# Norm gains of keys, values, queries and gate multiplied into the weight split, one transposed x for four products

## Chip, core and metric

The kernel runs on one core of a Trainium2 chip. The metric is the device time of one execution in microseconds, taken as the median of several runs. Five engines work side by side, each through its own list of instructions in order: TensorE (PE in the profile, its weight loads PEld), VectorE (DVE), ScalarE (ACT), GpSimd (POOL) and SyncE (SP, which here only starts transfers). They wait for each other through semaphores.

## Reference

Two blocks of a decoder are computed one after the other, on 256 tokens of width 1024. The part that the change touches is the second layer of the first block: keys and values come from one normed x, queries and gate from another. Both norms divide the same x by the same root mean square, and differ only in the gain vector.

```python
def rms_norm(x, g):
    xf = x.astype(jnp.float32)
    y = xf * lax.rsqrt(jnp.mean(xf * xf, axis=-1, keepdims=True) + EPS)
    return (y * g.astype(jnp.float32)).astype(x.dtype)
...
            kv_in = rms_norm(x, kv_norm)
            k_all, v_all = jnp.split(kv_in @ w_kv, 2, axis=-1)
            k_sh = rms_norm(split_heads(k_all), k_norm)
            v_sh = split_heads(v_all)
            h = rms_norm(x, b_norm[j])
            q, z = jnp.split(h @ b_w_in[j], 2, axis=-1)
            q = rms_norm(split_heads(q), b_q_norm[j])
            o = stick_breaking_attention(q, k_sh, v_sh)
            x = x + (o * jax.nn.silu(z)) @ b_w_out[j]
        x = x + (p[i] @ ple_w[i]) * jax.nn.sigmoid(x @ ple_gate_w[i])
```

After it come the second block's two attentions (called moba and mla), an MLP, a state-space mixer and a second MLP.

## The kernel before

**Split products.** Each large product runs as three matmuls (lines 591, 592, 593): high part of the activations times high part of the weights, high times low, low times high. A weight block of 1024 x 512 arrives in the tile ring in two halves, of 128 x 2048 each (four slabs of 128 input rows by 512 columns). For each half ScalarE writes the high part (whi, line 1035), VectorE then subtracts it from the block and writes the low part (wlo, line 1356). Both have three buffers (PARTS), so half g can be made when TensorE is done with half g-3. A half is 24 matmuls. The helper refill(name, half) in the two engines' lists makes the half that lies three ahead of the one named; the refill stands in the list between other work, and its place there sets the order. The wait first_used says that TensorE is done with a block's first half, low_made that a half is ready for TensorE.

**Transposed activations.** turn() has TensorE transpose x, two chunks of 128 columns and both token tiles to a unit, four units to a tensor (line 584). ScalarE reads a unit's bank and writes hT_hi (line 1018 with a gain as its scale, line 1015 without), VectorE reads the same bank and writes hT_lo (line 1347). Four such tensors of units stand in the stage at hand: "kv" (x with kv_norm), "qz" (x again, with b_norm), then "k" and "q" (the normed keys and queries of the heads, copied out by both engines in turn, lines 1006 and 1336). The order on TensorE is: turn kv, products k and v, turn qz, turn k, product q, product zb (the gate), turn q, then stick-breaking attention. The reciprocal root mean square is applied to the products as they are copied out (line 993), so the transposed x holds the gain alone.

**Head norms.** For keys, and later for queries, VectorE squares (line 1575), sums (line 1580) and finishes the mean, GpSimd takes the power (rsh, line 1855), VectorE scales (line 1585) and signals heads_normed. The chain stands in VectorE's list behind the low part of the second half of block v1 (for keys) or zb1 (for queries), and ahead of the next two refills.

**Banks.** There are eight PSUM banks. The class Units writes the plan: each result unit takes the next bank in turn (or a fixed one where the attention loops name it), and records which unit held the bank before and which engine empties it. TensorE waits for that in begin(). A unit more or less in the plan therefore shifts the bank of every later unit that is numbered in turn, against those with a fixed bank. Fixed banks are used by the units of the three attention loops: stick-breaking (logits and loga in 0 to 5, stick_out in 6 and 7), moba and mla (scores in 0 to 3, probsT in 4 and 5, soft_out in 6 and 7). The MLP takes its f1 units from banks 4 to 7 in turn and its sums from 0 to 3.

## Time and profile before

| | |
|---|---|
| median of 3 runs | 1003.29 us (1002.31 to 1003.59) |
| the profiled execution | 1003.81 us |
| its span, first to last instruction | 1002.0 us |
| PE busy | 910.1 us, 91% |
| DVE busy | 577.8 us, 58% |
| ACT busy | 440.2 us, 44% |
| mean granted TensorE clock | 0.951 of 2.4 GHz |

The stage at hand runs from about 134 us (turn kv) to 238 us (first logits). Stick-breaking attention ends at 284 us, moba starts at 396 us, mla at 432 us, the first MLP at 476 us. A timeline row gives start, duration, engine, line, operation, output and inputs, count of merged instructions, and in brackets how long the engine had been idle before and who released it. Consecutive instructions overlap a little, so that of a merged row the duration divided by the count is the distance at which one follows the other.

### The profile page before, as it was taken

What the parts mean: (1) busy time and instruction counts of PE and PEld (TensorE: products, weight loads), DVE (VectorE), ACT (ScalarE), POOL (GpSimd) and SP (SyncE); (2) the same over time, 40 slices, a digit from 0 to 9 for tenths busy, and PEclk for the clock granted to TensorE, in tenths of its full rate; (3) what the DMA queues carried; (4) which work ended last, traced back from release to release, by engine and by line L of the source; (5) the groups of instructions that cost most, each with busy time, mean ns of one, the idle gap of its engine ahead of it and who ended that gap; (6) DMA issues with size and microseconds to landing.
All of it is one profiled execution on the core that took longest, in us unless ns stands there. A gap on an engine that the chain in (4) does not pass through costs nothing.

```text
span 1002.0 us, 11908 instructions
## 1 busy us (share of the span) xinstructions
PE 910.1 (91%) x4907; PEld 750.9 (75%) x4907; DVE 577.8 (58%) x754; ACT 440.2 (44%) x552; POOL 134.2 (13%) x72
## 2 busy tenths in 40 slices
PE   3999999898999999999999999996519989999998
PEld 3888778786887886787788888875517878888886
DVE  3585465654244675767677777762482464545553
ACT  4443564555743646254444444422305454444441
POOL 1000000101000011213044444440020000000000
PEclk9999999997999999599999999997857999999999
DMA  9526555451023643206355555479525655555531
GB/s 351 195 85 210 185 202 200 139 197 43 1 79 126 220 146 118 107 22 210 126 189 200 189 200 189 158 116 106 157 116 210 186 168 180 182 190 188 171 124 42
DMA packets 66783, 155.84 MB, mean 156 GB/s; under 512 B 2937, under 2 KB 6618, under 8 KB 66474
## 3 DMA queue, kind: packets, MB, share of 16 engines
q1 hardware_dynamic: 64000, 145.89, 45.4%
q0 software_dynamic: 2224, 7.67, 2.2%
q10 hardware_dynamic: 506, 1.52, 0.4%
q8 instruction: 39, 0.64, 0.3%
q14 instruction: 14, 0.11, 0.0%
HBM read 146.69 MB, written 7.34 MB: 154 GB/s over the span
## 4 chain that ended last, share of the span: by engine, by line
PE 81%; DVE 10%; ACT 3%; issue 2%; DMA 2%; POOL 2%; ACTq 0%; SPq 0%; POOLq 0%
PE bank L591 22%; PE bank L593 22%; PE bank L592 21%; POOL rsh L1855 2%; PE bank L584 2%; DVE wlo L1356 2%; PE bank L686 1%; PE bank L845 1%; PE bank L715 1%; DMA vrows<-in_vecs 1%; PE bank L930 1%; PE bank L960 1%; DVE aux L1810 1%; DVE aux L1812 1%; PE bank L727 1%
## 5 line engine op out<-in xcount | busy, mean ns | idle before, releaser
L1356 DVE TENSOR_TENSOR wlo<-ring,whi 128x2048 fp32r<-128x2048 f32 (+1 forms) x122 | 288.4, 2368 | 208.6 <-ACT whi L1035 208.6
L1035 ACT ACTIVATE whi<-ring 128x2048 fp32r<-128x2048 f32 (+1 forms) x124 | 236.8, 1911 | 274.0 <-PE bank L593 239.4
L591 PE MATMUL bank<-whi,hT_hi 128*128 128x512 f32 (+1 forms) x736 | 290.9, 395 | 9.3 <-DVE hT_lo L1347 7.3
L593 PE MATMUL bank<-whi,hT_lo 128*128 128x512 f32 (+1 forms) x736 | 288.1, 391 | 0.0
L592 PE MATMUL bank<-wlo,hT_hi 128*128 128x512 f32 (+1 forms) x736 | 288.0, 391 | 0.0
L591 PEld LDWEIGHTS bank<-whi,hT_hi 128*128 128x128 f32 x736 | 139.7, 190 | 38.6 <-DVE hT_lo L1347 5.8
L593 PEld LDWEIGHTS bank<-whi,hT_lo 128*128 128x128 f32 x736 | 139.5, 190 | 28.9
L592 PEld LDWEIGHTS bank<-wlo,hT_hi 128*128 128x128 f32 x736 | 139.8, 190 | 27.7
L591 PE MATMUL bank<-whi,hidT_hi 128*128 128x512 f32 x256 | 100.7, 393 | 1.1 <-DVE hidT_lo L1753 1.1
L593 PE MATMUL bank<-whi,hidT_lo 128*128 128x512 f32 x256 | 99.8, 390 | 0.0
L592 PE MATMUL bank<-wlo,hidT_hi 128*128 128x512 f32 x256 | 99.6, 389 | 0.0
L591 PEld LDWEIGHTS bank<-whi,hidT_hi 128*128 128x128 f32 x256 | 48.0, 188 | 12.5 <-issue 2.9
L593 PEld LDWEIGHTS bank<-whi,hidT_lo 128*128 128x128 f32 x256 | 48.0, 188 | 10.2
L592 PEld LDWEIGHTS bank<-wlo,hidT_hi 128*128 128x128 f32 x256 | 48.1, 188 | 9.8
L1244 ACT ACTIVATE aux<-bank 128x512 f32<-128x512 f32 x32 | 19.2, 599 | 45.9 <-PE bank L593 45.9
L1855 POOL TENSOR_TENSOR rsh<-msh,half_neg 128x16 f32<-128x16 f32 (+1 forms) x6 | 22.5, 3742 | 125.6 <-DVE msh L1581 125.6
L1851 POOL TENSOR_TENSOR rstd<-ms,half_neg 128x2 f32<-128x2 f32 x4 | 2.8, 707 | 267.9 <-DVE ms L1371 267.9
L993 ACT ACTIVATE work<-bank,rstd 128x512 f32<-128x512 f32 (+1 forms) x32 | 21.8, 686 | 34.2 <-PE bank L593 34.1
L960 PE MATMUL bank<-ring,aux 64*32 64x128 f32 x256 | 11.4, 415 | 27.9 <-DVE aux L1819 27.9
L1760 DVE TENSOR_TENSOR aux<-bank,aux 128x512 f32<-128x512 f32 x32 | 22.0, 688 | 18.8 <-ACT aux L1244 18.8
L960 PEld LDWEIGHTS bank<-ring,aux 64*32 64x32 f32 x256 | 10.0, 166 | 29.1 <-DVE aux L1819 28.1
L1483 DVE TENSOR_TENSOR aux<-pb,bb 128x512 f32<-128x512 f32 x16 | 27.6, 1762 | 0.0
(244 smaller groups left out, 1016.2 us busy)
## 6 DMA issues: line engine op xcount, KB each, us to landing
ring<-in_w_ff SPq DMA_DIRECT2D x64, 1024.0 KB, 5.3
ring<-in_a_w_in SPq DMA_DIRECT2D x8, 1024.0 KB, 8.3
ring<-in_ple_gate_w SPq DMA_DIRECT2D x8, 1024.0 KB, 5.0
ring<-in_w_kv SPq DMA_DIRECT2D x8, 1024.0 KB, 6.5
ring<-in_b_w_in SPq DMA_DIRECT2D x8, 1024.0 KB, 5.0
ring<-in_w_glu SPq DMA_DIRECT2D x8, 1024.0 KB, 6.0
ring<-in_w_in SPq DMA_DIRECT2D x6, 1024.0 KB, 5.8
ring<-in_a_w_out SPq DMA_DIRECT2D x4, 1024.0 KB, 5.1
```

Source lines behind the costliest of these rows:

```text
L584: last = pe.transpose(b[0:width, cc * S + t * P:cc * S + t * P + P], src[:, t, c * width:(c + 1) * width], ident)
L591: pe.matmul(bank_cols, high[:, at[0], at[1]], w_high, start=first, stop=False)
L592: pe.matmul(bank_cols, high[:, at[0], at[1]], w_low, start=False, stop=False)
L593: return pe.matmul(bank_cols, low[:, at[0], at[1]], w_high, start=False, stop=last)
L960: last = pe.matmul(b[32 * q:32 * q + 32, s * P:(s + 1) * P], states[rows, 0:NC, 8 * m + 4 * r + s], wr[rows, 8 * q + 4 * r + s, :], start= ...
L993: act.activation(dst, b[:, :] if src is None else src, func, scale=scale).then_inc(act_emptied, 1)
L1035: act.activation(whi[at], ring[:, slot[name], cols], ACT.Copy).then_inc(high_made, 1)
L1244: act.activation(hid[:, t, :], b[:, :], ACT.Relu).then_inc(relu_ready, 1)
L1356: dve.tensor_tensor(wlo[at], ring[:, slot[name], cols], whi[at], ALU.subtract).then_inc(low_made, 1)
L1483: dve.tensor_tensor(at[:, 4 * r:4 * r + 4], ai[:, 4 * r:4 * r + 4], other, ALU.mult)
L1760: dve.tensor_tensor(hid[:, t, :], b[:, :], hid[:, t, :], ALU.mult).then_inc(dve_emptied, 1)
L1855: pool.tensor_tensor(rsh[:, 0:n], msh[:, 0:n], half_neg[:, 0:n], ALU.pow).then_inc(headr_ready, 1)
```

## The change

The gains kv_norm and b_norm are no longer applied to the transposed x but to the weights as they are split: row r of a weight block is multiplied by entry r of the gain. In a half, each slab of 512 columns has a gain column of its own, so one instruction on 128 x 2048 becomes four on 128 x 512, on ScalarE (scale operand) and on VectorE (scalar_tensor_tensor: block times gain minus high part) alike. This is done for the 16 halves of k, v, q and zb. Since the transposed x then holds no gain, the units of "qz" go (16 transposes on TensorE, 8 activations, 8 VectorE instructions), and q and zb use the transposed "kv", which is copied without a gain.

```diff
@@ plan()
     gemm(u, "v", 2, "a")
-    turned_in_two(u, "qz")
     turned(u, "k")
@@ tensor engine
-            turn("qz", x)
             turn("k", k_tok, ready=lambda k: pe.wait_ge(heads_normed, 1))
             for nb in range(2):
-                product("q", nb, ("q", nb), turned_by="qz")
+                product("q", nb, ("q", nb), turned_by=None)
@@ shared
+        gained = {"k": "kv_norm", "v": "kv_norm", "q": "b_norm", "zb": "b_norm"}
@@ scalar engine, fill(g)
+                if name[0] in gained:
+                    for kk in range(4):
+                        n = slice(512 * kk, 512 * kk + 512)
+                        ins = act.activation(whi[at][:, n], ring[:, slot[name], cols][:, n], ACT.Copy,
+                                             scale=gain(gained[name[0]], 4 * (g % 2) + kk))
+                    ins.then_inc(high_made, 1)
+                    return
                 act.activation(whi[at], ring[:, slot[name], cols], ACT.Copy).then_inc(high_made, 1)
...
-            turned_high("kv", "kv_norm")
+            turned_high("kv", None)
...
-                if nb:
-                    turned_high("qz", "b_norm")
                 tokens_out("v", nb, v_tok, 1)
@@ vector engine, fill(g)
+                if name[0] in gained:
+                    for kk in range(4):
+                        n = slice(512 * kk, 512 * kk + 512)
+                        ins = dve.scalar_tensor_tensor(out=wlo[at][:, n], in0=ring[:, slot[name], cols][:, n],
+                                                       scalar=gain(gained[name[0]], 4 * (g % 2) + kk),
+                                                       in1=whi[at][:, n], op0=ALU.mult, op1=ALU.subtract)
+                    ins.then_inc(low_made, 1)
+                    return
...
-            turned_low("kv", "kv_norm")
+            turned_low("kv", None)
...
             refill(("v", 1), 0)
-            turned_low("qz", "b_norm")
             turned_out("k", [(kT, "k_norm", True)])
```

On TensorE, between the end of product v and the start of product q, there stood before (first the transposes of x, then those of the normed keys, then the first matmul of q; a bracket lists the semaphores waited for):

```order
L584 MATMUL bank<-cst,x 128x128 [waits act_emptied]
L584 MATMUL bank<-cst,x 128x128 x3
...
L584 MATMUL bank<-cst,work 128x128 [waits heads_normed,act_emptied]
L584 MATMUL bank<-cst,work 128x128 x3
...
L591 MATMUL bank<-whi,hT_hi 128x512 [waits low_made,dve_emptied]
```

and stands now (line 584 is 585 there, 591 to 593 are 592 to 594; the first row is the last matmul of v):

```order
L594 MATMUL bank<-whi,hT_lo 128x512
L585 MATMUL bank<-cst,work 128x128 [waits heads_normed,act_emptied]
L585 MATMUL bank<-cst,work 128x128 x3
...
L592 MATMUL bank<-whi,hT_hi 128x512 [waits low_made,act_emptied]
L593 MATMUL bank<-wlo,hT_hi 128x512
```

The transposes of x are gone, and product q no longer waits for VectorE's reading of them.

At the end of stick-breaking attention, where the output is transposed for b_out, TensorE's list read before (line 741 is the last matmul of stick_out 3):

```order
L741 MATMUL bank<-work,aux 128x64
L584 MATMUL bank<-cst,h 128x128 [waits dve_emptied,act_emptied]
L584 MATMUL bank<-cst,h 128x128 x3
...
L584 MATMUL bank<-cst,h 128x128 [waits dve_emptied]
L584 MATMUL bank<-cst,h 128x128 x3
L591 MATMUL bank<-whi,hT_hi 128x512 [waits low_made,dve_emptied,act_emptied]
```

and reads now:

```order
L741 MATMUL bank<-work,aux 128x64
L585 MATMUL bank<-cst,h 128x128 [waits dve_emptied]
L585 MATMUL bank<-cst,h 128x128 x3
L585 MATMUL bank<-cst,h 128x128 [waits dve_emptied,act_emptied]
L585 MATMUL bank<-cst,h 128x128 x3
...
L592 MATMUL bank<-whi,hT_hi 128x512 [waits low_made,dve_emptied,act_emptied]
```

The same four units are transposed; their banks, and with them the waits, are others. The four units fewer in the plan shift the banks by four at these places (bank: unit that held it before, and the engine that empties it):

| unit | before | now |
|---|---|---|
| T k 0 to 3 | 3 to 6: v (ACT) | 7, 0, 1, 2: k (ACT) |
| q 0,0 and 0,1 | 7, 0: T qz 0, 1 (DVE) | 3, 4: v 0 (ACT) |
| T o1 0 | 3: loga 15 (ACT) | 7: stick_out 3 (DVE) |
| T o1 1 to 3 | 4, 5, 6: loga 10, 11 (ACT), stick_out 2 (DVE) | 0, 1, 2: loga 12, 13, 14 (ACT) |
| moba scores 0 | 0: ukv 1,1 (ACT) | 0: uq 1,1 (ACT) |
| moba scores 1 to 3 | 1, 2, 3: uq (ACT) | 1, 2, 3: ukv 0,0 to 1,0 (ACT) |
| mla scores 0 | 0: T kmla 3 (ACT) | 0: T qmla 3 (ACT) |
| mla scores 1 to 3 | 1, 2, 3: T qmla 0, 1, 2 | 1, 2, 3: T kmla 0, 1, 2 |
| first f1, token tile 0 | 4: T ffn 3 (DVE) | 4: w_o 1,1 (DVE) |
| first f1, token tile 1 | 5: w_o 0,0 (DVE) | 5: T ffn 0 (DVE) |

T ffn 0 to 3 are the transposed x of the first MLP, f1 its first product; ukv and uq are the small products ahead of moba.

## Rows read from the trace of the kernel before

**Rows 1.** The page: busy time of the engines, share of the span, instructions.

```profile
PE 910.1 (91%) x4907; PEld 750.9 (75%) x4907; DVE 577.8 (58%) x754; ACT 440.2 (44%) x552; POOL 134.2 (13%) x72
```

**Rows 2.** Groups by form, ACT: form, count, busy us, mean ns, idle before.

```profile
L1035 ACT ACTIVATE whi<-ring 128x2048 fp32r<-128x2048 f32 x122 | 233.6, 1916 | 270.6 <-PE bank L593 236.0 <-DMA ring<-in_w_glu 9.0 <-DMA ring<-in_ple_gate_w 8.8
L993 ACT ACTIVATE work<-bank,rstd 128x512 f32<-128x512 f32 x30 | 20.6, 692 | 33.7 <-PE bank L593 33.6
...
L993 ACT ACTIVATE aux<-bank 128x512 f32<-128x512 f32 x12 | 7.2, 598 | 21.4 <-PE bank L930 15.9 <-PE bank L686 5.5
```

**Rows 3.** Groups by form, DVE, the same columns.

```profile
L1356 DVE TENSOR_TENSOR wlo<-ring,whi 128x2048 fp32r<-128x2048 f32 x120 | 284.7, 2376 | 206.2 <-ACT whi L1035 206.2
...
L1777 DVE SCALAR_TENSOR_TENSOR x<-bank,inv,x 128x512 f32<-128x512 f32 x8 | 6.0, 751 | 16.7 <-PE bank L593 16.7
...
L1396 DVE SCALAR_TENSOR_TENSOR aux<-aux 128x64 f32<-128x64 f32 x1 | 0.2, 225 | 0.0
L1439 DVE TENSOR_TENSOR aux<-aux 128x64 f32<-128x64 f32 x1 | 0.2, 225 | 0.0
```

**Rows 4.** Timeline of DVE ahead of product k.

```profile
130.92 2.29 DVE L1356 TENSOR_TENSOR wlo<-ring,whi 128x2048 fp32r<-128x2048 f32 x1 [2.12 <-ACT whi L1035]
133.13 0.68 DVE L1550 TENSOR_TENSOR sig<-sig,aux 128x512 f32<-128x512 f32 x1
...
134.99 0.69 DVE L1550 TENSOR_TENSOR sig<-sig,aux 128x512 f32<-128x512 f32 x1 [0.45 <-ACT sig L1108]
```

**Rows 5.** The chain that ended last, 135 to 240 us: start, duration, what.

```profile
135.71 0.70 DVE x L1557
...
164.94 1.93 ACT whi L1035
166.89 2.29 DVE wlo L1356
...
181.76 4.40 DVE wlo L1356 x2
186.16 1.58 DVE hT_lo L1347 x4
187.83 0.47 PE bank L591
...
215.40 1.93 ACT whi L1035
```

**Rows 6.** Timeline around the end of stick-breaking attention.

```profile
284.41 1.92 PE L584 MATMUL bank<-cst,h 128*128 128x128 f32 x16
284.61 0.69 DVE L1624 TENSOR_TENSOR h<-bank,work 128x512 f32<-128x512 f32 x1 [3.68 <-PE bank L741]
```

**Rows 7.** Timeline, start of moba, then of mla.

```profile
391.54 3.60 PE L786 MATMUL bank<-ring,aux 128*128 128x512 f32 x8
...
396.06 0.48 PE L801 MATMUL bank<-pT,sig 64*128 64x128 f32 x2 [0.93 <-ACT work L1206]
...
428.98 2.62 DVE L1336 TENSOR_SCALAR work<-bank,vcols 96x256 f32<-96x256 f32 x6 [0.51 <-PE bank L584]
432.04 0.49 PE L801 MATMUL bank<-work 96*128 96x128 f32 x2 [0.92 <-ACT work L1006]
```

**Rows 8.** Timeline, start of the first MLP: DVE, then PE.

```profile
473.02 3.23 DVE L1347 SCALAR_TENSOR_TENSOR hT_lo<-bank,vcols,hT_hi 128x256 fp32r<-128x256 f32 x8 [0.62 <-ACT hT_hi L1018]
...
476.30 0.80 PE L591 MATMUL bank<-whi,hT_hi 128*128 128x512 f32 x1 [2.69 <-DVE hT_lo L1347]
```

**Rows 9.** Stretches: us, then busy (count) of PE, PEld, DVE, ACT, POOL, PEclk, DMA share, GB/s.

```profile
181.00:188.00 7.00, 4.19 (x34) 3.57 (x33) 7.00 (x8) 6.36 (x13) 0.00 (x0) 1.00 0.39 128
...
237.40:247.60 10.20, 9.95 (x32) 7.48 (x33) 1.80 (x4) 5.33 (x11) 0.00 (x0) 0.50 0.31 104
...
472.90:476.30 3.40, 0.71 (x8) 0.47 (x6) 3.23 (x8) 3.40 (x8) 0.00 (x0) 0.99 0.59 241
476.30:479.70 3.40, 3.40 (x8) 2.72 (x9) 2.55 (x3) 2.85 (x5) 0.00 (x0) 0.51 0.00 0
```

## The prediction

> **What bounds the kernel.** I read the page first: TensorE is busy for 910.1 of 1002.0 us [rows 1], so a gain of 2 us has to come from time in which TensorE stands still or runs at its lower clock, or from instructions taken off it. The 16 transposes taken away are 1.75 us of it. Then the chain that ended last, for the stage that changes [rows 5]: it leaves TensorE three times. Ahead of k it runs through the last update of x (135.71 + 0.70). From 164.94 it runs through the high and low part of the second half of v1, the head norm of the keys, the low parts of q's two halves, and two units of hT_lo, to the first matmul of q at 187.83. From 215.40 it runs through the same for the queries, up to the logits. So in this stage VectorE and ScalarE set two of the three stretches, and work added to them is not hidden there. Elsewhere there are three buffers: a half takes TensorE 5.5 us (five of them from 187.83 to the release at 215.40 [rows 5]), so the next one in a buffer is due 11 us after its release, and is made in 1.93 + 2.29 us [rows 5]: there, added work is hidden up to some 6 us. Last I read what TensorE waits for where the banks shift: the ends and starts of the attention loops and the first MLP [rows 6 to 8].
>
> **The dearer split.** High part: one instruction of 1.92 us on 2048 columns becomes four on 512 with a gain as scale. The nearest row is the copy-out with a scale from a tile, 0.692 us on 512 [rows 2]; back to back it overlaps by about 0.09, so four take some 2.5 us: a = 0.6 us more. Bounded below by the 512 without a scale, 0.598, four in 2.07: 0.15 more; above by no overlap, 2.77: 0.85. Low part: four of the form "times a column, then with a tensor", 0.751 us on 512 [rows 3], overlap 0.08: 2.8 us against 2.29, d = 0.5 us more. Below: if the form cost no more than a plain 512 of 0.68 [rows 4], four in 2.5, 0.2 more; above without overlap, 3.0: 0.7.
>
> The row of 0.751 reads one operand from a bank, where the changed instruction reads both tensors from SBUF. The one pair of rows for that is small: on 64 columns, both from SBUF, this form took 225 ns, and the plain two-tensor form 225 ns too [rows 3], so at that size there is no sign of a lower rate. The Trainium skill, "Vector Engine (DVE) Microarchitecture Reference", section "Points that are easy to get wrong", speaks against this change: the form with two SBUF sources that are not bf16 runs at half the throughput. By that page each low part would take about twice as long; the trace does not agree at 64 columns, and shows no larger case. It is the second rival below.
>
> **The stage, step by step** (positive is later than before).
> 1. Before k: the low part of k0's second half, 130.92 to 133.21, stands ahead of the gate work [rows 4]. It starts a later and lasts d longer. Of that 0.54 was slack, since without the wait for ScalarE the instruction of 134.99 could have started at 134.45. So x is ready, and product k starts, at a + d - 0.54 = 0.56 later. The copies of "kv" without gains get cheaper, but nothing waits for them.
> 2. Products k and v run without a gap: each half is made in 5.3 instead of 4.2 us and due after 11. The second half of v1 is released 0.56 later and costs a + d = 1.1 more; the head norm behind it is as before. heads_normed comes 1.66 later, at 183.4.
> 3. TensorE ends v near 181.9 (the release at 164.94, three halves more, and 0.56) and stands until 183.4; it transposes k in 1.9 us, as 16 transposes took in [rows 6], to 185.4. q's first half is low at 181.76 + 1.66 + 2.8 = 186.1, and q starts at 186.3. Before, its low part was ready at 184.0 but q waited for the second unit of hT_lo until 187.83, its banks having been those of qz 0 and 1. So q starts 1.5 to 1.6 **earlier**: in symbols 2a + 3d - 4.28.
> 4. Products q and zb run through. The second half of zb1 starts 1.56 earlier, costs 1.1 more, and the norm of the queries behind it is as before: the logits start 3a + 4d - 4.28 = **0.5 earlier**. From the low bounds of a and d it is 3.0 earlier, from the high ones 1.1 later.
>
> So the folding itself is almost given back. TensorE's 1.75 us of transposes were done in time in which it would have waited.
>
> **The banks.** Four units fewer move all later ones.
> 5. End of stick-breaking: T o1 0 now takes the bank of stick_out 3. TensorE started it at 284.41, right behind its last matmul, while VectorE reads that bank from 284.61 to 285.30 [rows 6]. It now waits for 285.4: **1.0 later**; nothing behind it has slack, since T, ScalarE's high and VectorE's low part follow one another.
> 6. Start of moba: the first scores waited 0.93 for ScalarE to empty ukv 1,1, until 396.02, though the last ukv was done at 395.14 [rows 7]. They now need uq 1,1, whose matmuls lie ahead of the first ukv at 391.54. ScalarE's next work needs the first maximum, and VectorE's needs these scores, so the whole chain moves: **0.9 earlier**.
> 7. Start of mla: the first scores waited for ScalarE to empty T kmla 3, until 432.0, 0.92 after the transposes had ended. They now need T qmla 3, four units earlier in ScalarE's list, and T kmla 0, which VectorE ends with the fourth of its six instructions from 428.98, at 430.7 [rows 7], before the last transpose: **0.8 earlier**.
> 8. First MLP: f1 waited for the bank of T ffn 3, so for all 8 instructions of hT_lo, 473.02 to 476.25, and started at 476.30 after 2.69 idle [rows 8]. It now needs T ffn 0 alone, two of them, ready at 473.9; the next unit comes at 474.7 and is due at 475.3. Its weights are ready, their low parts standing ahead of the eight in VectorE's list. **2.3 earlier**. What ScalarE and VectorE do next for f1 is released by TensorE's own matmuls, so nothing takes this back.
> 9. The clock: at 473 to 476.3 TensorE was busy for 0.7 of 3.4 us, and in the next 3.4 us it was granted 0.51, the lower level of 1.2 GHz [rows 9]. Without the wait there is no such lull. At half speed for 3.4 us it lost **1.7**.
>
> Sum for the profiled execution: -0.5 + 1.0 - 0.9 - 0.8 - 2.3 - 1.7 = -5.2, 1003.8 - 5.2 = 998.6 us (its span is 1002.0, and 1.8 lie around it, unchanged). The median is 1003.3, 0.5 below the profiled execution; whether the lower clock fell at 476 in all runs is not known, so against the median I take it at two thirds: 1003.3 - 3.5 - 1.1 = 998.7. I predict **998.7 us**.
>
> **Rivals.**
> - *The bank gains do not arrive* (10%). Were something else due just behind at steps 6 to 8, only the folding and step 5 would be left: 1003.3 - 0.5 + 1.0 = 1003.8, and with one of the three 1000.4 to 1003. For it: moba and mla are chains over three engines with small waits everywhere. Against: the named releaser was the last to come in each, and idle time stood on all engines.
> - *The low part at half rate* (4%), the one that ends slower. Per column the plain low part takes 1.1 ns (2.29 us on 2048), so a piece would take 0.751 + 0.55 = 1.3 us, four 5.0, d = 2.7. Then step 4 gives 1.8 + 10.8 - 4.28 = 8.3 later instead of 0.5 earlier: 998.7 + 8.8 = 1007.5. It decides from d = 1.8 on, where the gain of the banks is used up. VectorE would be busy for 5.0 of each 5.5 us in k to zb.
> - *The clock falls at the keys' transposes* (5%). TensorE is busy for only 1.9 of the 4.4 us from 181.9 to 186.3. Before, it was busy for 4.19 of 7 us there and kept the full clock [rows 9]. A lower stretch lasted 3.4 or 10.2 us in this trace and would cost 1.7 to 5: 1000.4 to 1003.7.
> - *Cheap pieces* (8%): with the low bounds of a and d the folding brings 3.0 instead of 0.5: 996.2.
>
> **Numbers.** The forecast with its own spread (a and d between bounds, the clock at step 9 lost or not) holds 73% and spans 996.9 to 1000.6. The range of eight in ten reaches over the cheap pieces and a bank gain that is missing in part: 996.2 to 1001.2. A change under 0.2% (2 us) is about what a measurement of this kernel cannot tell from none. Below 1001.3 lie the forecast, the cheap pieces and part of the clock's and the banks' case: faster 0.85. Within 0.2% most of the rest of these: 0.11. Slower: 0.04.
>
> **What would show it.** High parts of k to zb in groups of four, about 2.5 us, low parts about 2.8; product q starting near 186.3, the logits 0.5 us earlier than before; the transposes of o1 with an idle time of 1.0 released by VectorE's h; no wait for ScalarE at the first scores of moba and mla; f1 starting 0.4 us after the transposes, with the full clock behind it. The forecast is wrong if the low part takes over 4 us, if TensorE's idle time at f1 stays at 2 us or more, or if the PEclk row falls between 182 and 190 us.

## The result and the profile after

| | before | after | predicted |
|---|---|---|---|
| median | 1002.92 us (1002.31 to 1003.59, 4 runs) | 995.71 us (995.03 to 996.31, 4 runs) | 998.7 (996.2 to 1001.2) |
| ratio | | 0.9929 [0.9902, 0.9956] | 0.9954 |
| profiled execution, its span | 1003.81, 1002.0 | 996.31, 994.5 | 998.6 for the profiled one |

The change is faster, as forecast, but by 7.2 us and not by 4.6, and so 0.5 us below the range. In words first: the steps at the stage itself and at the banks came out nearly as worked out, but for the clock. In the profiled pair a further 3.3 us were gained 450 us behind the change, in the state-space mixer, where the prediction had looked for nothing. Why TensorE lost time there before is shown below by experiment; how much of it the medians hold is not.

The page after (answers [rows 1]): TensorE has 16 instructions fewer and is busy 2.2 us less.

```profile
PE 907.9 (91%) x4891; PEld 749.5 (75%) x4891; DVE 581.2 (58%) x794; ACT 446.9 (45%) x588; POOL 134.3 (13%) x72
```

Groups by form after (answers [rows 2, 3]; form, count, busy us, mean ns of one, idle before it). The 16 halves are now 64 pieces on each engine. A piece of the low part, both tensors in SBUF, takes 747 ns, where the same form with one operand in a bank took 751.

```profile
L1369 DVE TENSOR_TENSOR wlo<-ring,whi 128x2048 fp32r<-128x2048 f32 x104 | 248.1, 2389 | 170.6 <-ACT whi L1042 170.6
L1042 ACT ACTIVATE whi<-ring 128x2048 fp32r<-128x2048 f32 x106 | 202.9, 1916 | 244.9 <-PE bank L594 207.0 <-DMA ring<-in_ple_gate_w 12.2 <-DMA ring<-in_w_glu 10.5
...
L1364 DVE SCALAR_TENSOR_TENSOR wlo<-ring,vcols,whi 128x512 fp32r<-128x512 f32 x64 | 43.7, 747 | 31.2 <-ACT whi L1038 31.1
L1038 ACT ACTIVATE whi<-ring,vcols 128x512 fp32r<-128x512 f32 x64 | 40.9, 712 | 22.0 <-PE bank L594 22.0
```

The timeline of VectorE ahead of product k (answers [rows 4]): the low part of k0's second half now takes 2.74 us instead of 2.29 and starts 0.40 later, and the gate work behind it no longer waits for ScalarE.

```profile
131.32 2.74 DVE L1364 SCALAR_TENSOR_TENSOR wlo<-ring,vcols,whi 128x512 fp32r<-128x512 f32 x4 [2.28 <-ACT whi L1038]
...
135.30 0.68 DVE L1563 TENSOR_TENSOR sig<-sig,aux 128x512 f32<-128x512 f32 x1
136.02 0.69 DVE L1570 TENSOR_TENSOR x<-x,sig 128x512 f32<-128x512 f32 x1
```

The chain that ended last (answers [rows 5]; start, duration, what). The same road as before: the split of the second half of v1, the head norm, one half of q low, then product q, at 187.55. The step through hT_lo is gone.

```profile
166.85 2.57 ACT whi L1038 x4
169.45 2.74 DVE wlo L1364 x4
172.19 2.21 DVE aux L1588
...
182.46 2.29 DVE work L1598
184.75 2.66 DVE wlo L1364 x4
187.41 0.14 issue
187.55 0.47 PE bank L592
...
215.38 2.57 ACT whi L1038 x4
```

The end of stick-breaking attention (answers [rows 6]), the starts of moba and mla ([rows 7]) and of the first MLP ([rows 8]), four pieces of timelines. T o1 now waits for VectorE's h, 0.79 of idle time. The first scores of moba and of mla and f1 start right behind the work in front of them.

```profile
284.27 0.69 DVE L1636 TENSOR_TENSOR h<-bank,work 128x512 f32<-128x512 f32 x1 [3.68 <-PE bank L741]
285.02 1.97 PE L585 MATMUL bank<-cst,h 128*128 128x128 f32 x16 [0.79 <-DVE h L1636]
```

```profile
392.21 3.60 PE L786 MATMUL bank<-ring,aux 128*128 128x512 f32 x8
395.74 0.49 PE L801 MATMUL bank<-pT,sig 64*128 64x128 f32 x2
```

```profile
428.82 1.91 PE L585 MATMUL bank<-cst,work 128*96 128x128 f32 x16
430.56 0.39 PE L801 MATMUL bank<-work 96*128 96x128 f32 x2
```

```profile
469.91 2.10 PE L585 MATMUL bank<-cst,x 128*128 128x128 f32 x16
472.44 0.47 PE L592 MATMUL bank<-whi,hT_hi 128*128 128x512 f32 x1 [0.43 <-DVE hT_lo L1352]
```

The stretches (answers [rows 9]; busy us and count of PE, PEld, DVE, ACT, POOL, then PEclk, DMA share, GB/s). Behind 473 the clock now stays full. Behind 138.0, at the start of product k, it is at 0.52, the lower level, which it was not before.

```profile
134.60:138.00 3.40, 1.48 (x13) 1.25 (x11) 3.33 (x8) 1.56 (x4) 0.00 (x0) 0.98 0.81 255
138.00:141.40 3.40, 3.40 (x9) 2.62 (x8) 1.78 (x6) 3.40 (x7) 0.00 (x0) 0.52 0.14 54
...
469.60:473.00 3.40, 2.97 (x22) 2.33 (x21) 2.27 (x6) 2.45 (x7) 0.00 (x0) 1.00 0.87 277
473.00:476.40 3.40, 3.40 (x16) 2.80 (x15) 2.63 (x6) 3.40 (x5) 0.00 (x0) 1.00 0.08 34
```

**Where the time went.** I took marks on TensorE at which both traces do the same thing, and subtracted the lengths between them (us, profiled executions):

| from, to | before | after | difference | forecast |
|---|---|---|---|---|
| start, second half of T kv | 136.55 | 136.86 | +0.31 | +0.56 |
| to the first matmul of q | 51.28 | 50.69 | -0.59 | -2.1 |
| to the first logits | 49.82 | 51.18 | +1.36 | +1.1 |
| to T o1, its wait included | 46.76 | 46.29 | -0.47 | +1.0 |
| to the first probsT of moba | 115.88 | 114.95 | -0.93 | -0.9 |
| to T o2, behind mla | 48.08 | 46.82 | -1.26 | -0.8 |
| to the middle of the first MLP | 42.18 | 38.32 | -3.86 | -4.0 |
| to the regrouping in the state-space mixer | 194.06 | 194.01 | -0.05 | 0 |
| to line 960, in the same mixer | 63.55 | 60.23 | **-3.32** | 0 |
| to TensorE's last wait, 15 us before the end | 238.82 | 240.12 | +1.30 | 0 |

In the row of T o1 the new wait is inside, but the low stretch at the start of attention was 10.2 us long before (237.4 to 247.6, [rows 9]) and 6.8 us after (240.3 to 247.1), which gives back about 1.6. After, 3.4 us more at the lower level stand ahead of this row, at 233.5 to 236.9, in the transposes of the queries. They cost nothing in the row of the first logits: from q to the logits it is 51.18 us in spare16, which has such a stretch, and 51.22 in all_three, which has none (both kernels stand below). The one large row that the forecast has at nothing is the state-space mixer.

**What is in that row.** TensorE's timeline at line 930, before:

```profile
701.50 0.66 PE L916 MATMUL bank<-cst,aux 128*128 128x128 f32 x4
702.09 0.95 PE L930 MATMUL bank<-work 128*32 128x128 f32 x7
707.15 3.64 PE L930 MATMUL bank<-work 128*32 128x128 f32 x25 [4.12 <-issue]
```

and after:

```profile
697.31 1.99 PE L930 MATMUL bank<-work 128*32 128x128 f32 x24
701.40 1.06 PE L930 MATMUL bank<-work 128*32 128x128 f32 x8 [2.10 <-issue]
702.40 0.66 PE L916 MATMUL bank<-cst,aux 128*128 128x128 f32 x4
```

"Issue" means that the profile shows nothing that TensorE waited for. Line 930 is a group of 128 equal matmuls. Before, TensorE stops after 103 of them for 4.12 us and has 25 left, which take 3.64 us at the lower clock (at the full clock 24 of them take 1.99). After, it stops after 120 for 2.10 us and has 8 left, 1.06 us. The page has a queue that nobody in the kernel feeds: q8, kind "instruction", 39 packets of 16 KB. I take it for TensorE's list coming in: 4907 pairs of weight load and matmul over 39 packets is 126 pairs each. So it comes in blocks, one a packet; where one block ends and the next begins is called an edge here. In the kernel before, the share of each queue from 686.5 to 703.5 us, and, in the second fence, in the 2.5 us behind that, inside the stop (a share adds up the packets' own times, and can pass 100%):

```profile
q1 hardware_dynamic: 1180, 2.00, 109.3%
issues: line engine op xcount, KB each, median us to landing
ring<-scratch_taps SPq DMA_DIRECT2D x2, 256.0 KB, 20.0
```

```profile
q1 hardware_dynamic: 132, 0.23, 83.3%
q8 instruction: 1, 0.02, 4.2%
```

For 17 us the transfers of scratch_taps (eight of 256 KB, issued from 683.3 on, landing up to 20.9 us after their issue) fill all 16 DMA engines, and no instruction packet moves. One moves at 704.0, a good microsecond before the DMA engines fall idle; it takes 1.68 us, and TensorE goes on 1.5 us behind its end. Up to 704.0 TensorE had done 3434 pairs, which is the edge at which it had stopped:

```profile
0.00:704.00 704.00, 652.93 (x3434) 536.32 (x3434) 423.99 (x508) 325.95 (x447) 125.23 (x70) 0.96 0.49 154
```

So the theory for these 3.3 us, **theory A**: TensorE's list comes in blocks; the block whose edge lies in line 930 is held up by the scratch_taps transfers; TensorE can go on only some 16.8 us after the first matmul of line 908, whatever lies in front of the edge. Sixteen transposes taken out of the list, some 520 us earlier, let 17 more matmuls pass before the edge, and 17 fewer are left behind the stop. (That it is 17 and not 16 I did not follow up; with 16 put back the edge stands at 104.) The Trainium skill, "Runtime: NRT & Kernel Launch", section "Instruction fetch mechanics", says that an engine's list is refilled in 16 KiB blocks of 256 instructions by a queue of its own, and that crossing a block's edge is mostly hidden. The trace agrees on the block (16 KB a packet, and 126 pairs of two are 252 instructions), and shows an edge that isn't hidden, at up to 4.25 us. I hadn't weighed that page.

### The profile page after: what moved, and what is told of

Its sections match the earlier page's. It is cut to its first block, busy times and chain, and to the rows that moved or that the text cites. A ratio compares the mean times of both kernels' runs of the same rounds, so it can differ in the third digit from the quotient of the medians.

```text
span 994.5 us, 11950 instructions
## 1 busy us (share of the span) xinstructions
PE 907.9 (91%) x4891; PEld 749.5 (75%) x4891; DVE 581.2 (58%) x794; ACT 446.9 (45%) x588; POOL 134.3 (13%) x72
## 4 chain that ended last, share of the span: by engine, by line
PE 81%; DVE 10%; ACT 3%; DMA 2%; issue 2%; POOL 2%; ACTq 0%; SPq 0%; POOLq 0%
PE bank L592 22%; PE bank L594 22%; PE bank L593 22%; POOL rsh L1867 2%; PE bank L585 2%; PE bank L687 1%; PE bank L845 1%; DMA vrows<-in_vecs 1%; PE bank L960 1%; PE bank L715 1%; DVE wlo L1364 1%; PE bank L930 1%; DVE aux L1824 1%; DVE aux L1830 1%; PE bank L727 1%
## 5 line engine op out<-in xcount | busy, mean ns | idle before, releaser
L1369 DVE TENSOR_TENSOR wlo<-ring,whi 128x2048 fp32r<-128x2048 f32 (+1 forms) x106 | 251.9, 2379 | 173.1 <-ACT whi L1042 173.0
L1042 ACT ACTIVATE whi<-ring 128x2048 fp32r<-128x2048 f32 (+1 forms) x108 | 206.1, 1910 | 248.4 <-PE bank L594 210.4
L1364 DVE SCALAR_TENSOR_TENSOR wlo<-ring,vcols,whi 128x512 fp32r<-128x512 f32 x64 | 43.7, 747 | 31.2 <-ACT whi L1038 31.1
L594 PEld LDWEIGHTS bank<-whi,hidT_lo 128*128 128x128 f32 x256 | 48.1, 188 | 10.2
L1038 ACT ACTIVATE whi<-ring,vcols 128x512 fp32r<-128x512 f32 x64 | 40.9, 712 | 22.0 <-PE bank L594 22.0
```

The lines of the kernel that those rows point to most:

```text
L594: return pe.matmul(bank_cols, low[:, at[0], at[1]], w_high, start=False, stop=last)
L1038: ins = act.activation(whi[at][:, n], ring[:, slot[name], cols][:, n], ACT.Copy, scale=gain(gained[name[0]], 4 * (g % 2) + kk))
L1042: act.activation(whi[at], ring[:, slot[name], cols], ACT.Copy).then_inc(high_made, 1)
L1364: ins = dve.scalar_tensor_tensor(out=wlo[at][:, n], in0=ring[:, slot[name], cols][:, n], scalar=gain(gained[name[0]], 4 * (g % 2) + kk), i ...
L1369: dve.tensor_tensor(wlo[at], ring[:, slot[name], cols], whi[at], ALU.subtract).then_inc(low_made, 1)
```

## Experiments

Every kernel was compared with the kernel before on its own chip; medians in us, runs in brackets, the ratio to before with its 95% interval. "Edge after" is the number of matmuls of the group of 128 that stand ahead of the edge: read from the stop where there is one, else worked out from the number of instructions added. "Stop" is the standstill there. "Stage" is the length from the regrouping (line 901 of before) to line 960. The last two are of the profiled execution, one for each kernel.

| kernel | median (lowest to highest, n) | before there | ratio | edge after | stop, us | stage |
|---|---|---|---|---|---|---|
| banks_only | 997.46 (990.4 to 997.6, 5) | 1003.15 | 0.992 [0.9891, 0.995] | 103 | none | 57.49 |
| fold_only | 999.12 (997.86 to 1001.31, 5) | 1003.15 | 0.9969 [0.9951, 0.9987] | 120 | 2.79 | 60.56 |
| f1_only | 998.6 (990.45 to 1001.41, 10) | 1003.15 | 0.9947 [0.992, 0.9974] | 103 | 4.14 | 63.75 |
| spare16 | 994.29 (991.95 to 995.53, 4) | 1003.15 | 0.991 [0.9895, 0.9926] | 104 | 4.25 | 62.78 |
| after_again | 995.32 (993.08 to 998.99, 6) | 1002.6 | 0.9924 [0.9897, 0.9951] | 120 | 3.31 | 60.99 |
| head16 | 996.72 (989.39 to 1002.34, 12) | 1002.6 | 0.9935 [0.9908, 0.9963] | 104 | 2.03 | 58.48 |
| head64 | 993.17 (992.1 to 997.03, 6) | 1002.6 | 0.9905 [0.9877, 0.9933] | 56 | none | 56.41 |
| o1_undone | 995.14 (991.82 to 1000.0, 6) | 1002.6 | 0.9921 [0.9891, 0.9952] | 120 | 3.23 | 61.03 |
| before_head48 | 996.9 (995.56 to 1000.02, 6) | 1002.69 | 0.9947 [0.9926, 0.9967] | 55 | none | 56.81 |
| k_order | 997.29 (992.31 to 998.63, 6) | 1002.69 | 0.9933 [0.9907, 0.9959] | 120 | 2.27 | 60.50 |
| k_order_o1 | 994.35 (992.75 to 998.7, 6) | 1002.69 | 0.9923 [0.9897, 0.9948] | 120 | 3.48 | 61.72 |
| all_three | 989.61 (988.28 to 994.51, 6) | 1002.69 | 0.9876 [0.9853, 0.9899] | 64 | none | 56.33 |
| half_taps | 996.0 (994.76 to 999.99, 12) | 999.55 | 0.997 [0.9951, 0.9989] | 103 | none | 56.86 |
| edits_p0 | 994.63 (993.04 to 998.83, 12) | 999.55 | 0.9963 [0.9942, 0.9984] | 120 | 3.39 | 61.26 |
| edits_p16 | 998.4 (991.74 to 1000.98, 12) | 999.55 | 0.9982 [0.996, 1.0005] | 104 | 2.09 | 59.16 |
| edits_p56 | 991.18 (988.89 to 994.86, 6) | 999.55 | 0.9924 [0.99, 0.9949] | 64 | none | 56.34 |

### The two halves of the change apart

Both use the turn of the banks in the plan: four added to it puts all later units where they stand in the other kernel.

banks_only is the kernel before with

```diff
     turned(u, "q")
+    u.turn += 4
```

> The kernel before with nothing folded; only the plan's turn is advanced by four banks ahead of stick-breaking attention, so that o1, moba, mla and the first MLP get the banks of the changed kernel. Theory A (the gain is the banks, and a separate 3 us in the state-space stage comes from 16 transposes fewer in TensorE's list, which moves the place where it runs out of fetched instructions): o1 1.0 later, moba 1.0, mla 1.3 and f1 3.9 earlier as the two traces show, 5.2 in all, about 997.8 us, and TensorE still stands for about 4 us, named issue, after 103 of the 128 matmuls of the line 930 loop. Theory B (the folding itself brings the missing part): 1000 or more. Theory C (the 3 us are a matter of where the low clock falls, which follows the earlier arrival): 994 to 996, with the stall shortened to about 2 us here too.

fold_only is the changed kernel with the banks of before:

```diff
     gemm(u, "v", 2, "a")
+    u.turn += 4
     turned(u, "k")
```

> The changed kernel with four turns of the bank plan kept where the qz units were, so that every later unit has the bank it had before. Theory A: the folding costs or gives under 2 us up to the logits (0.5 earlier without, 1.2 later with a low clock at k's start), and the 3 us of the state-space stage remain, since the 16 transposes are gone: 999.5 to 1001.5 us, with the stall after about 120 matmuls of line 930. Theory B: 998 or less. Theory C: 1002.4 to 1004, stall after 103.

f1_only is the kernel before with `u.turn += 4` ahead of turned_in_two(u, "o2") alone, so that only the first MLP and what follows has the new banks.

> The kernel before, with the plan's turn advanced by four ahead of o2 alone, so only o2, w_o and the first MLP get the banks of the changed kernel. The prediction's step 8 and 9: f1 starts behind the first two instead of all eight instructions of hT_lo, 2.3 earlier, and the clock does not fall there, 1.7 more if it fell in every run before: 998.9 us. If the low stretch at 476 was this one execution's: 1000.6. Theory C would add a gain in the state-space stage: 996 to 997.

The banks alone brought 0.8% and the folding alone 0.3%. In the traces the waits go exactly where their banks go: the wait of 0.93 at moba, of 0.92 at mla and the 2.69 at f1 are in fold_only as before and in banks_only not; f1_only has the first two and lacks the third: from T o2 to the middle of the first MLP it takes 38.34 us where before took 42.18. The folding's 0.3% was more than the 0.5 us that I gave it. At the first logits fold_only stands 0.17 behind before, at the regrouping 0.49, and only at line 960 2.5 ahead: its gain is made in the state-space mixer, where it stops after 120 matmuls like the changed kernel, and not in the stage that it changes. banks_only, whose list is as long as that of before, was to stop for 4 us, and has no stop in its profiled execution; three of its five runs lie at 997.5 and two at 990.4 (the profiled one) and 992.2. The two halves do not add up within this scatter: 5.7 and 4.0 us of median, where the whole change brought 7.2.

### The length of TensorE's list

spare16 is the changed kernel with 16 transposes more, into a bank that is overwritten, ahead of the wait for the normed keys, where TensorE stands idle:

```diff
-            turn("k", k_tok, ready=lambda k: pe.wait_ge(heads_normed, 1))
+            def keys_ready(k):
+                if k == 0:
+                    b = bank(("T", "k", 0))
+                    for n in range(16):
+                        pe.transpose(b[:, n % 4 * P:n % 4 * P + P], x[:, n % 2, n % 8 * P:n % 8 * P + P], ident)
+                pe.wait_ge(heads_normed, 1)
+
+            turn("k", k_tok, ready=keys_ready)
```

> The changed kernel with 16 transposes of x put into TensorE's wait for the normed keys (they write the bank that the real ones then overwrite; extra work, same result), which restores the number of instructions in its list. The wait there is 1.8 us and they take 1.75, so they cost about nothing in place. Theory A: the stall in the line 930 loop moves back to after 103 matmuls and costs the 2.5 to 3 us again: 998 to 999 us. Theories B and C: 995.2 to 996.2, the stall where the changed kernel has it.

head16 and head64 put matmuls of constants at TensorE's start, while it waits for its first data; after_again is the changed kernel on their chip.

```diff
+            pe.wait_ge(masks_ready, 1)
+            for _ in range(8):
+                pe.matmul(ps[7][:, 0:16], allneg[:, :], allneg[:, 0:16], start=True, stop=True)
             pe.wait_ge(tables_landed, 16)
```

> The changed kernel once more, on the chip of the next three. All theories: about 7 us below the kernel before, standing for 2.1 us in the state-space mixer with 120 of 128 matmuls of a group done.

> The changed kernel with 16 matmul instructions more (8 products of constants, 16 columns) at TensorE's start, in time in which it has nothing to do. Nothing else of the computation is changed. Theory A (TensorE's list has the length of before again, so the standstill in the state-space mixer is back after 103 matmuls of the group, lasts 4.1 us and costs 3 us): 2.5 to 3.5 us slower than the changed kernel, 999. Rival (the standstill is not set by the place in the list, its length is chance): within 1 us of the changed kernel and the standstill after 120 matmuls or elsewhere.

> The same with 64 matmul instructions more at TensorE's start. Theory A: the standstill comes after 120 - 64 = 56 matmuls of the group (about 4 us earlier on the clock), and if what it waits for comes at a time set by the transfers of the stage, it is longer, 6 us or more: 999 to 1003. Rival: as the changed kernel, 996, with the standstill after 120 matmuls.

The place obeyed: 120 in the changed kernel, 104 with 16 more in either way (8 of the last 32 done, 24 left), and with 64 more no stop in line 930. head16 (its line 933 is line 930):

```profile
691.89 1.06 PE L933 MATMUL bank<-work 128*32 128x128 f32 x8
694.98 2.00 PE L933 MATMUL bank<-work 128*32 128x128 f32 x24 [2.03 <-issue]
```

My figures for the time did not obey. spare16 stops for 4.25 us and its stage takes 62.78 us, 2.6 more than in the changed kernel, and yet its median is 994.3 where theory A had 998 to 999: by the ratios it is 1 to 2 us faster than the changed kernel, not 3 slower. head64 was to stop longer, and did not stop there (0.50 us at line 944, its 947), being 2.1 us faster than the changed kernel. In it and the three other traces with the edge at 55 to 64 a packet moves 17 to 18.5 us ahead of line 908's transposes, and the transfers are issued from 7 us ahead of them: the packet is through before they begin. And head16 lies at 1.4 above the changed kernel where I had 3, with runs from 989 to 1002. So the place was shown, and its worth in the median left open.

### The kernel before with another edge

before_head48 is the kernel before with the same edit and 24 matmuls (48 instructions).

> The kernel before the change, with 48 matmul instructions more (24 products of constants, 16 columns) at TensorE's start, in time in which it has nothing to do. Nothing else. Theory A (a block of TensorE's list is fetched late; the block's edge stood after 103 of the 128 matmuls of the state-space group, now after 55, as close as the 56 with which the standstill was gone): no standstill at line 930; the state-space stage, 63.55 us before, takes 56 to 58; median 4 to 6 us below the kernel before. Rival (the standstill of before belongs to the kernel before, its time or its clock, and not to the place in the list): it stays, median within 1 us of before.

```profile
701.61 2.46 PE L933 MATMUL bank<-work 128*32 128x128 f32 x32
704.00 0.66 PE L919 MATMUL bank<-cst,aux 128*128 128x128 f32 x4
```

No stop at line 930 (933 here), the stage 56.81 instead of 63.55, and 5.8 us off the median of a kernel in which nothing but idle time was filled. The standstill belongs to the place and not to the change.

### What holds the packet back, and what a place is worth

half_taps is the kernel before, with half of each of the eight transfers of the second Toeplitz block; it leaves the other half of that block out of its result:

```diff
                     for j, src in parts:
-                        sp.dma_start(ring[GI * j:GI * j + GI, slot[name], :].rearrange("p (g s n) -> p g s n", g=2, s=4), src)\
+                        dst = ring[GI * j:GI * j + GI, slot[name], :].rearrange("p (g s n) -> p g s n", g=2, s=4)
+                        if name[1] == 1:
+                            dst, src = dst[:, 0], src[:, 0]
+                        sp.dma_start(dst, src)\
```

> The kernel before the change, in which the eight transfers of the second Toeplitz block fetch half of their rows; the second half of this block is left out of the computation (old numbers stand there). TensorE's list is as before, so the block's edge stands after 103 of the 128 matmuls. Theory A (the instruction transfer waits behind these eight, which land 20.9 us after their issue at the latest): they land some 9 us earlier, the instruction transfer gets through before TensorE needs it, no standstill, state-space stage 57 to 58 us, median 4 to 6 below the kernel before. Rival (the edge at 103 costs its 4 us whatever the transfers do): as before.

The list is that of before, so the edge stands after 103. The instruction packet moves at 694.0, 5.9 us after the start of line 908's transposes, where before it moved 13.7 us after it. TensorE had then done 3353 pairs, 81 fewer than the edge at 3434, and there is no stop. Stretches of half_taps, and its queues from 693.9 to 696 us:

```profile
0.00:694.00 694.00, 644.74 (x3353) 529.75 (x3355) 423.99 (x508) 322.15 (x442) 125.20 (x70) 0.96 0.48 155
```

```profile
q8 instruction: 1, 0.02, 5.1%
q1 hardware_dynamic: 14, 0.01, 3.4%
```

The DMA share is 1.09 from 687 to 693 us, 0.92 in the next microsecond and 0.15 in the one behind 694.0, so the packet moves as the shorter transfers end. banks_only has the one packet that moved as early with whole transfers (4.1 us after the transposes), and there the share was still 1.1. It is the scratch_taps transfers that hold the packet, and it was asked for 81 pairs ahead of the edge at the latest. The median fell by 3.6 where I had 4 to 6; before itself lay 3 us lower on this chip than on the others.

The last three are one kernel (the changed one with the two edits of the next part) with 0, 16 and 56 instructions more at the start, on the same chip. edits_p0 is the kernel k_order_o1 of the next part, edits_p56 its all_three.

> The changed kernel with the two other edits (low part behind the gate work, T o1 with its old bank) and no instructions added: edge after 120 matmuls. Both: standstill ends 16.7 to 17.0 us after the first matmul at line 908's transposes, stage 60 to 62 us.

> The same with 16 instructions of constants more at TensorE's start: edge after 104. Theory A with the end of the standstill fixed by the transfers: the end is where it was, but 16 matmuls more lie behind it, 1.4 us at the full clock and up to 3 with the clock low behind the longer standstill, unless the instruction transfer slips in early: median 0 to 3 above edits_p0.

> The same with 56: edge after 64, no standstill there, stage 56 to 57 us. Theory A: median 3 to 5 below edits_p0, 990. Rival (the 989.6 measured for this kernel was one chip's): as edits_p0.

Edge after 120: 994.6; after 104: 998.4; after 64: 991.2. All three in the order of theory A, but the kernels with 0 and 16 are not told apart: their runs overlap (993.0 to 998.8 and 991.7 to 1001.0), as do the intervals of their ratios. That of the kernel with 56 barely touches the one with 0. Over all traces of the study TensorE goes on 16.7 to 17.0 us after the first transpose of line 908 in ten of the twelve with a stop, with the edge at 103, 104 or 120, so the end of the stop is set by the transfers. In the two others (head16 and edits_p16, 14.1 and 14.7 us) the packet moved 10.5 and 11.2 us after that transpose, and in banks_only 4.1 us after it and with no stop. All three of these have their edge at 103 or 104: there the packet sometimes slips through early. That may be why kernels with that edge scatter (runs over 13 us in head16, 11 in f1_only, 9 in edits_p16, 7 in banks_only), which was not shown, with one trace of each. One trace of such a kernel settles nothing.

The same traces say what the edge is worth. With the edge at 120 the stage took 60.2 to 61.7 us, 60.9 in the mean of seven traces. With the edge at 103 or 104 and whole transfers it took 57.5 to 63.7, and the mean of the six is 60.9 too: 62.8 to 63.7 where the packet is held to the end, 57.5 to 59.2 where it slips through. The 3.3 us of the profiled pair are the difference from one held trace, and no mean gain. In the medians 103 or 104 against 120 was 1.4 and 3.8 us slower in two comparisons, and 1 to 2 faster in spare16. I have no better figure than this spread. An edge at 55 to 64 is worth more, and is the firm result: 56.3 to 56.8 us of stage in four traces, and 5.8 us of median in the kernel before.

### The other two places

o1_undone gives T o1 its old bank: `u.turn += 4` ahead of turned_in_two(u, "o1") and once more ahead of turned_in_two(u, "x1", (0, 1)), after which the turn is as in the changed kernel.

> The changed kernel with the banks of the transposes of o1 and of the two after the output product as before the change, so that T o1 0 takes a bank that ScalarE has long emptied; all later banks as in the changed kernel. All theories: the 0.79 idle for VectorE's h at 284 is gone, and everything behind it is 0.8 to 1.0 us earlier: the marks at the first scores of moba, mla and f1 by that much, the end too, unless the standstill in the state-space mixer takes it back (it stays after 120 matmuls). Median 0.8 below the changed kernel on the same chip.

The idle time of 0.79 is gone, and so is the low stretch of 3.4 us that stood at 282 in after_again. But at gate1's transposes it stands 0.69 later than after_again. Its clock was low from 231.5 to 248.5 without a break, that of after_again from 230.9 to 234.3 and from 237.7 to 244.6. The median is the same (995.1 and 995.3), where I had 0.8 less. The wait was as forecast; what it is worth could not be told from what the clock does.

k_order moves one call in VectorE's list behind the work that TensorE waits for, and k_order_o1 has both edits.

```diff
             for nb in range(2):
-                refill(("gate0", nb), 0)
+                if nb == 0:
+                    refill(("gate0", nb), 0)
                 for t in range(NT):
                     gate_in(("gate0", nb, t), t, nb, pl_tok[:, t, nb * 512:(nb + 1) * 512], None)
...
             turned_low("kv", None)
+            refill(("gate0", 1), 0)
             refill(("gate0", 1), 1)
```

> The changed kernel; on VectorE alone the low part of the second half of k's first block moves behind the gate work and behind the low units of x, so the four dearer pieces stand no longer ahead of x. Theory C (the lull of 1.92 us ahead of product k and the fall of the clock at 138 come from the dearer split in front of x): x is ready 0.6 us earlier, the lull is 1.3 us, and no low stretch starts at 136 to 138: 0.6 us in an execution whose clock did not fall, 2.3 where it did. Rival: VectorE is late for k's second half or for the root of x behind it, and TensorE stands 1 us or more inside product k: no gain. Median 0 to 1.5 below the changed kernel.

> The last one, and also the bank of T o1 0 as before the change. Both theories: another 0.8 us for T o1, unless the low stretch behind 232 or 238 us gets longer, as with the bank edit alone. Median 0.5 to 2 below the changed kernel.

> The last one, and also 56 matmul instructions of constants at TensorE's start, in its free time. Theory A: the edge of the block stands after 64 of the 128 matmuls, no standstill at line 930, the state-space stage takes 56 to 58 us: median 990 to 992, 3 us below the last one. Rival: as the last one.

VectorE's timeline in k_order, and TensorE's stretch there:

```profile
132.69 0.69 DVE L1570 TENSOR_TENSOR x<-x,sig 128x512 f32<-128x512 f32 x1
133.30 2.94 DVE L1352 SCALAR_TENSOR_TENSOR hT_lo<-bank,hT_hi 128x256 fp32r<-128x256 f32 x8
136.15 3.39 DVE L1364 SCALAR_TENSOR_TENSOR wlo<-ring,vcols,whi 128x512 fp32r<-128x512 f32 x5
```

```profile
131.30:134.70 3.40, 2.04 (x18) 1.79 (x17) 2.71 (x6) 2.09 (x5) 0.00 (x0) 1.00 0.00 0
134.70:138.00 3.30, 3.30 (x16) 2.73 (x15) 3.18 (x8) 3.30 (x7) 0.00 (x0) 1.00 0.00 0
```

The idle time ahead of product k is 1.36 again, in the middle of the transposes of x, and no low stretch follows: none in six traces with this order, against three of seven with the order of the change (after, fold_only, head64). Product k did not have to wait for the low part that now comes later. Alone the edit did not show in the median (997.3, runs from 992.3 to 998.6), and with the bank edit beside it the ratio is 0.9923, as that of the changed kernel. With all three edits the kernel runs at 989.6, a ratio of 0.9876 [0.9853, 0.9899] to before, and on a second chip at 991.2 and 0.9924 [0.99, 0.9949]. This is the fastest kernel of the study.

## Why the prediction was right in direction and wrong in size

**Prices of the split.** Right. High part 2.57 a half (a = 0.65, forecast 0.6), low part 2.74 where nothing overlaps it (d = 0.45, forecast 0.5). The rival at half rate is refuted: it had about 1.3 us a piece, and the 64 pieces took 747 ns each. The row on 64 columns was the right guide. The Trainium skill, "Vector Engine (DVE) Microarchitecture Reference", section "Points that are easy to get wrong", says that this form runs at half the throughput with two SBUF sources that are not bf16; the trace does not agree.

**Step 1**, k 0.56 later: x is ready at 136.71, 0.31 later, and the trace stood 0.26 ahead at 80 us already, so 0.57. Right. What it does to the clock I missed. The idle time of TensorE there grew from 1.36 to 1.92, and in the next 3.4 us the clock was at its lower level, which costs the 1.7 that I had worked out for such a stretch. The rival had the fall at the keys' transposes; there it stayed full, and it fell in front of product k. (The rival's "3.4 or 10.2 us" for a low stretch was not all that the trace before held: others lasted 6.9, 27.3 and 37.6 us.)

**Steps 2 and 3**, q 1.5 to 1.6 earlier, so 2.1 earlier against T kv: measured 0.59 earlier with the low stretch in between. In spare16, whose clock did not fall, it is 49.09 us from T kv to q against 51.28, 2.19 earlier. Right but for the clock.

**Step 4**, the logits: a + d = 1.1 more between q and the logits, measured 1.36, beside 0.33 that is an idle time of ScalarE ("issue") ahead of the split at 215.38 that I did not have.

**Step 5**, T o1 1.0 later: 0.79, and the banks did it, since banks_only has the same 0.79 and o1_undone none. The 1.6 of clock that came back in the same row hid it.

**Steps 6 and 7**: moba 0.9 forecast, 1.0 measured (0.99 from gate1's transposes to the first probsT). mla 0.8 forecast, 1.26 measured: the first scores now start before TensorE's transposes have ended in the trace's account, so the whole wait of 0.92 went, and 0.3 more that I can't assign. I had kept 0.1 of it for T kmla 0, which was done in time.

**Steps 8 and 9**, f1 and its clock: 4.0 forecast for an execution that loses the low stretch, 3.86 measured. For the median I had taken two thirds of the clock's 1.7. That was wrong: the low stretch behind the wait at 476 is in all four traces that have the wait (before, fold_only, before_head48, half_taps) and in none of the fourteen that lack it. That is 0.6 us of the 2.6 by which the median was missed.

**The step that failed** is the sentence behind step 4, that the 16 transposes were "done in time in which it would have waited", and cost nothing. That is true of their time. But they are also 16 pairs in TensorE's list, and taking them out moved every later edge of a block by 16. One of these edges stood where TensorE stopped for 4.12 us, with the clock low behind it. That term, absent from the sum, is -3.3 in the profiled pair: 17 matmuls fewer behind the stop are 1.4 at the full clock (24 in 1.99 us), and most of the rest is the clock behind the stop (25 in 3.64 us before). Against the forecast of -5.2 for the profiled execution the rows of the table give -3.3 here, +1.5 at product k (the clock), -1.5 ahead of T o1 (the clock), +1.3 behind line 960 (from there to the next block's transposed x the mean granted clock was 0.82 over 65.9 us, before 0.86 over 64.6), -0.5 at mla and +0.2 in the rest: -7.5. The clock's surprises come to +1.3 against the -3.3 of the state-space mixer; with the -0.3 of the rest that is the error of the profiled execution, -2.3. For the median, 2.0 us of the error are left when the 0.6 of step 9 is taken off. That the mixer gave them fits, but is not shown: spare16 got the stop back and lost no time in its median, and the mean stage is the same with the edge at 103 or 104 as at 120.

The trace before had a hint, in the list of TensorE's waits: 4.1 us at line 930 with "issue" as what ended it, the only such wait of TensorE's matmuls there. I read only the stages that the diff and the banks touch.

## What to carry to other kernels

A change to an engine's list also moves the edges of the blocks in which the list comes in. Look for idle time with "issue" as its end on the busiest engine; if the instruction queue's packet moves at the end of a stretch with the DMA share full (here 1.09), the edge can be moved off it by filling idle time with instructions, or the transfers can be made smaller. Price it from several runs: one trace of an edge that lies close can show the stop whole, in part or not at all. When a wait goes that had a low clock behind it, take that clock whole (here it was there with the wait in four of four traces); when dearer work goes in front of a lull, ask whether the clock falls there too, and put the new work behind what TensorE waits for.

## What was not expected of the hardware

- An instruction packet of 16 KB waits behind data transfers: eight transfers of 256 KB held it until TensorE had stood for 2.0 to 4.25 us, in 12 of 18 traces. In the kernel before it took 1.68 us itself, where 37 of the 39 took 0.88 to 1.32.
- The clock's low time at the start of attention differed between executions of one kernel: edits_p0 was at the lower level from 230.8 to 254.7 us, 23.9 us, and k_order_o1, the same kernel on another chip, from 237.3 to 247.5, 10.2 us. It moved traces by more than the wait of 0.8 us under test, and what sets its length stayed open.
